# Odd layer of a hybrid decoder: values of four heads at once, tokens on partitions

## The reference

```python
h = rms_norm(x, attn_norm_g[1])
q, f, i, g = jnp.split(h @ odd_w_in[0], 4, axis=-1)      # each 256 x 2048: 16 heads of 128
f = lb + (1 - lb) * sigmoid(f); log_f = log(f); k = 1 - f
# per head, causal, in chunks: b = cumsum(log_f)
attn[t, s] = sum_d q[t, d] * k[s, d] * exp(b[t, d] - b[s, d])   # s <= t
o = attn @ i                                                    # i: the head's values, 256 x 128
o = rms_norm(o, norm_g) * silu(g)
mix = o @ odd_w_out[0]
```

## Time and profile before

| | |
|---|---|
| median of 3 runs | 2486.32 us (2485.87 to 2486.61) |
| the profiled execution, its own time | 2485.35 us |
| its span from first to last instruction | 2483.6 us |
| PE, DVE, ACT, POOL busy, share of the span | 99%, 74%, 50%, 20% |
| odd heads: products of head 0 to products of head 15 | 1283.01 to 1661.67 us |
| granted PE clock while PE works | 1.00 |

### The profile page before, as it was taken

One profiled execution on the slowest core, in us unless ns is written; L12 is line 12 of the kernel. 1 busy time (PEld: TensorE's weight loads), 2 busy tenths in 40 slices (PEclk: granted clock), 3 DMA queues, 4 the chain that ended last, 5 costly groups with the idle time before them and its releaser, 6 DMA issues.

```text
span 2483.6 us, 45860 instructions
## 1 busy us (share of the span) xinstructions
PE 2466.9 (99%) x16576; PEld 2161.3 (87%) x16576; DVE 1830.0 (74%) x3028; ACT 1237.7 (50%) x1798; POOL 504.0 (20%) x436
## 2 busy tenths in 40 slices
PE   9999999999999999999999999999999999999998
PEld 8888888888888888888888888888888888888887
DVE  7888888766665666567989999997666556655665
ACT  5666666544433444344655656555444434443444
POOL 0123322222200221022212322213222012200220
PEclk9999999999999999999999999999999999999999
DMA  7333333455555555554554444445455555555553
GB/s 274 121 138 139 121 121 121 170 186 186 194 194 187 186 186 190 192 192 170 189 184 169 169 165 172 153 163 215 178 188 187 202 186 186 186 203 185 187 195 127
DMA packets 65570, 438.32 MB, mean 176 GB/s; under 512 B 9408, under 2 KB 10816, under 8 KB 15808
## 3 DMA queue, kind: packets, MB, share of 16 engines
q1 hardware_dynamic: 61632, 436.29, 49.4%
q10 hardware_dynamic: 3840, 0.70, 0.1%
HBM read 434.87 MB, written 2.10 MB: 176 GB/s over the span
## 4 chain that ended last, share of the span: by engine, by line
PE 85%; DVE 8%; issue 4%; ACT 2%; DMA 1%; ACTq 0%; SPq 0%; DVEq 0%
PE acc L333 29%; PE acc L403 17%; PE mixer_banks L414 10%; PE acc L385 9%; PE acc L397 9%; PE acc L368 6%; DVE w_low L323 2%; DVE arena L1568 2%; DVE arena L446 1%; DVE arena L1556 1%; PE mixer_banks L1695 1%; PE acc L330 1%; DVE arena L1558 1%; DMA w_raw<-w_even 1%; PE mixer_banks L1783 0%
## 5 line engine op out<-in xcount | busy, mean ns | idle before, releaser
L318 ACT ACTIVATE w_high<-w_raw 128x1024 fp32r<-128x1024 f32 x831 | 863.3, 1057 | 892.5 <-PE acc L385 387.5
L323 DVE TENSOR_TENSOR w_low<-w_raw,w_high 128x1024 fp32r<-128x1024 f32 x832 | 1048.9, 1287 | 123.0 <-ACT w_high L318 121.7
L333 PE MATMUL acc<-h_split,w_high 128*128 128x512 f32 x3184 | 818.5, 396 | 1.0
L333 PEld LDWEIGHTS acc<-h_split,w_high 128*128 128x128 f32 x3184 | 575.3, 188 | 110.2 <-DVE arena L446 3.1
L565 POOL TENSOR_TENSOR arena<-arena,norm_scale 128x256 f32<-128x256 f32 x152 | 238.5, 1569 | 1340.9 <-DVE arena L446 1321.2
L446 DVE TENSOR_REDUCE arena<-acc 128x256 f32<-128x512 f32 x285 | 196.2, 688 | 289.3 <-PE acc L403 178.2
L403 PE MATMUL acc<-h_split,w_high 128*128 128x512 f32 x1376 | 328.2, 391 | 0.0
L403 PEld LDWEIGHTS acc<-h_split,w_high 128*128 128x128 f32 x1376 | 252.9, 188 | 48.9
L368 PEld LDWEIGHTS acc<-h_split,w_low 128*128 128x128 f32 x1824 | 263.7, 190 | 27.4
L368 PE MATMUL acc<-h_split,w_low 128*128 128x256 f32 x1824 | 273.4, 282 | 0.0
L333 PE MATMUL acc<-mix_split,w_high 128*128 128x512 f32 x752 | 185.7, 393 | 0.6 <-DVE x_residual L1140 0.6
(11 more groups left out here) (335 smaller groups left out, 2297.0 us busy)
## 6 DMA issues: line engine op xcount, KB each, us to landing
w_raw<-w_gu SPq DMA_DIRECT2D x176, 1024.0 KB, 4.8
w_raw<-w_odd SPq DMA_DIRECT2D x64, 1024.0 KB, 4.8
w_raw<-w_even SPq DMA_DIRECT2D x49, 1024.0 KB, 4.9
w_raw<-w_last SPq DMA_DIRECT2D x44, 1024.0 KB, 4.8
w_raw<-w_down SPq DMA_DIRECT2D x32, 1024.0 KB, 4.9
w_raw<-w_down SPq DMA_DIRECT2D x16, 768.0 KB, 4.3
w_raw<-w_odd_out SPq DMA_DIRECT2D x12, 1024.0 KB, 4.8
w_raw<-w_even_out SPq DMA_DIRECT2D x10, 1024.0 KB, 4.8
```

Of the source, the lines that this page charges most:

```text
L318: act.activation(wh[:, self.res, ks], raw[:, self.raw, ks], ACT.Copy).then_inc(high_done, 1)
L323: dve.tensor_tensor(wl[:, self.res, ks], raw[:, self.raw, ks], wh[:, self.res, ks].bitcast(F32), ALU.subtract).then_inc(low_done, 1)
L333: pe.matmul(acc[self.acc][:, 0:2 * T], wh[:, self.res, k], flat(both), start=k == 0, stop=stop)
```

## The change

Blocks of i are no longer one head each. Four blocks together hold the values of four heads, cut the other way: block v of a group has a quarter of the inner dimension for the 512 output columns of four heads, and is multiplied by tokens, in `by_tokens`, into two PSUM banks of the mixer that collect over four blocks. At a group's first head ACT copies both banks to `In` and multiplies by the norm's factor per token (`nrt`, which DVE makes once before the heads). So the values are not taken out by DVE, not scaled by POOL and not transposed on PE. A group's values must be complete at its first head: three blocks of the first group now run before head 0, head 0 runs the fourth and each following step a quarter of the next group. The loads keep their count, 64 blocks. Steps 0 to 12 have four blocks each, steps 13 and 14 three (f, g, q), with other cuts, and step 15 none as before. Steps 1 to 12 are a loop of three rounds over four steps; 0, 13, 14 and 15 are written out. The sigmoids of head 0 move ahead of three blocks' weight copies.

```diff
...
+        PRE = 6
+        GROUP_STEPS = NHG - 3
...
+        def odd_first(h):
...
+            return ODD + PRE + 4 * h - max(0, h - GROUP_STEPS) if isinstance(h, int) else None
...
+        def odd_block(h, u):
...
+            if isinstance(h, int):
+                first = odd_first(h)
+                return Block(first + u, kt=KT)
+            i, v = h
+            return Block(ODD + PRE + 4 + 4 * v + u, i, 16)
...
+        def odd_steps(eng, step):
...
+            step(0, 0)
+            with eng.Fori(0, 3) as i:
+                for v in range(4):
+                    step(4 * i + 1 + v, (1 + v) % 4, (i, v))
+            for h in range(GROUP_STEPS, NHG):
+                step(h, h % 4)
...
-            for u in range(3):
-                scale(ODD + u, (hf, hi, hg)[u], "hg_scaled")
-            with pool.Fori(0, NHG - 1) as h:
-                for u, dst in enumerate((hq, hf, hi, hg)):
-                    scale(Block(ODD + 3 + u, h, 4).n, dst, "hg_scaled")
-            scale(ODD + 4 * NHG - 1, hq, "hg_scaled")
+            scale(ODD, hf, "hg_scaled")
+            scale(ODD + 1, hg, "hg_scaled")
...
+            def odd_scales(h, _, at=None):
+                at = h if at is None else at
+                scale(odd_block(at, -1).n, hq, "hg_scaled")
+                if isinstance(h, int) and h == NHG - 1:
+                    return
+                scale(odd_block(at, 0).n, hf, "hg_scaled")
+                scale(odd_block(at, 2 if not isinstance(h, int) or h < GROUP_STEPS else 1).n, hg, "hg_scaled")
...
+            odd_steps(pool, odd_scales)
...
-            def odd_step(h, last=False):
-                blocks = [Block(ODD + 4 + u, h, 4) for u in range(5)]
+            def odd_step(h, quarter, where=None):
+                where = h if where is None else where
+                last = isinstance(h, int) and h == NHG - 1
+                grouped = not isinstance(h, int) or h < GROUP_STEPS
+                blocks = [odd_block(where, u) for u in range(5)]
...
-                act.wait_ge(S["hg_iT"], h + 1)
-                act.activation(flat(In), bank(5)[:, 0:256], ACT.Copy).then_inc(S["hg_In"], 1)
...
-                blocks[4].high(act, 0)
+                if grouped and quarter == 0:
+                    blocks[1].wait_half(act, 1)
+                    for th in range(2):
+                        act.activation(In[:, th], bank(2 + th), ACT.Copy, scale=nrt[:, th:th + 1]).then_inc(S["hg_In"], 1)
+                if grouped or last:
+                    blocks[4].high(act, 0)
...
-                blocks[4].high(act, 1)
+                if grouped or last:
+                    blocks[4].high(act, 1)
...
-                    act.wait_ge(S["hg_scaled"], 4 * h + 7)
+                    act.wait_ge(S["hg_scaled"], 3 * h + 5)
...
-            for u in range(3):
+            for u in range(PRE - 1):
...
-            act.wait_ge(S["hg_scaled"], 3)
-            gates()
-            with act.Fori(0, NHG - 1) as h:
-                odd_step(h)
-            odd_step(NHG - 1, last=True)
+                if u == 1:
+                    act.wait_ge(S["hg_scaled"], 2)
+                    gates()
+            act.wait_ge(S["hg_nrt"], 2)
+            odd_steps(act, odd_step)
...
-            def odd_step(h, last=False):
+            def odd_step(h, quarter, where=None):
+                where = h if where is None else where
+                last = isinstance(h, int) and h == NHG - 1
+                grouped = not isinstance(h, int) or h < GROUP_STEPS
...
-                    Block(ODD + 4 + half // 2, h, 4).low(dve, half % 2)
+                    if half < 8 or grouped or last:
+                        odd_block(where, half // 2).low(dve, half % 2)
...
-                        Block(ODD + 4 + u, h, 4).evacuate(dve, dst)
+                        odd_block(where, u if grouped else u // 2).evacuate(dve, dst, 2 if grouped and u == 0 else 1)
...
-                dve.wait_ge(S["hg_iT"], h + 1)
-                take(1, hi)
+                if last:
+                    take(1, None)
...
-            for u in range(3):
+            for u in range(PRE - 1):
...
-                Block(ODD + u).evacuate(dve, (hf, hi, hg)[u])
+                if u < 2:
+                    Block(ODD + u).evacuate(dve, (hf, hg)[u], (1, PRE - 2)[u])
...
+                if u == 1:
+                    dve.wait_ge(S["norm_rstd"], 3)
+                    turned = htmp.rearrange("p (c t) -> p c t", c=2)
+                    dve.tensor_tensor(turned, nrs.rearrange("p (c t) -> p c t", c=2), bc(ident, 2), ALU.mult).then_inc(S["hg_nrt"], 1)
+                    dve.wait_ge(S["hg_nrt"], 1)
+                    dve.reduce_sum(nrt, turned, AX.X).then_inc(S["hg_nrt"], 1)
...
-            with dve.Fori(0, NHG - 1) as h:
-                odd_step(h)
-            odd_step(NHG - 1, last=True)
+            odd_steps(dve, odd_step)
...
-            def value_turned(h):
...
-                pe.wait_ge(S["hg_scaled"], 4 * h + 2)
-                for c in range(2):
-                    prod = transposed(bank(5)[:, c * P:(c + 1) * P], hi[:, c * P:(c + 1) * P])
-                prod.then_inc(S["hg_iT"], 1)
...
-            def odd_step(h, last=False):
+            values = (bank(2), bank(3))
...
+            def odd_step(h, quarter, where=None):
+                where = h if where is None else where
+                last = isinstance(h, int) and h == NHG - 1
+                grouped = not isinstance(h, int) or h < GROUP_STEPS
+                first_cut, second_cut, third_cut, end_cut = (32, 46, 54, 64) if grouped else (24, 36, 42, 48)
...
-                        ks = range(max(first, part * HALF) % KT, (min(end, part * HALF + HALF) - 1) % KT + 1)
-                        Block(ODD + 4 + part * HALF // KT, h, 4).run(pe, ks, hs)
+                        this = odd_block(where, part * HALF // KT)
+                        if grouped and part == 2:
+                            this.by_tokens(pe, values, hs, (quarter + 3) % 4, 4)
+                        elif not grouped or part != 3:
+                            ks = range(max(first, part * HALF) % KT, (min(end, part * HALF + HALF) - 1) % KT + 1)
+                            this.run(pe, ks, hs)
...
                 prod.then_inc(S["hg_mm"], 1)
-                dense(32, 46)
+                dense(first_cut, second_cut)
                 out_half(2, 0)
...
                 pe.wait_ge(S["hg_AT"], 4 * h + 4)
-                waits(pe, h + 1, "hg_A01", "hg_In")
-                pe.matmul(bank(5)[:, 256:384], AM[:, 0], In[:, 0], start=True, stop=True)
-                pe.matmul(bank(5)[:, 384:512], A01, In[:, 0], start=True, stop=False)
-                pe.matmul(bank(5)[:, 384:512], AM[:, 1], In[:, 1], start=False, stop=True).then_inc(S["hg_o"], 1)
-                dense(46, 54)
+                pe.wait_ge(S["hg_A01"], h + 1)
+                if quarter == 0:
+                    pe.wait_ge(S["hg_In"], 2 if isinstance(h, int) else 2 * where[0] + 4)
+                mine = slice(quarter * P, quarter * P + P)
+                pe.matmul(bank(5)[:, 256:384], AM[:, 0], In[:, 0, mine], start=True, stop=True)
+                pe.matmul(bank(5)[:, 384:512], A01, In[:, 0, mine], start=True, stop=False)
+                pe.matmul(bank(5)[:, 384:512], AM[:, 1], In[:, 1, mine], start=False, stop=True).then_inc(S["hg_o"], 1)
+                dense(second_cut, third_cut)
                 out_half(3, 0)
...
                 prod.then_inc(S["hg_oT"], 1)
-                if not last:
-                    value_turned(h + 1)
-                dense(54, 64)
+                dense(third_cut, end_cut)
                 out_half(3, 1)
-            for n in range(2, 4):
-                for half in range(2):
-                    Block(ODD + n).products(pe, half, hs)
-            pe.wait_ge(S["hg_scaled"], 2)
-            for c in range(2):
-                first_turn = transposed(bank(5)[:, c * P:(c + 1) * P], hi[:, c * P:(c + 1) * P])
-            first_turn.then_inc(S["hg_iT"], 1)
-            with pe.Fori(0, NHG - 1) as h:
-                odd_step(h)
-            odd_step(NHG - 1, last=True)
+            for q in range(3):
+                Block(ODD + 2 + q).by_tokens(pe, values, hs, q, 4)
+            for half in range(2):
+                Block(ODD + PRE - 1).products(pe, half, hs)
+            odd_steps(pe, odd_step)
             pe.wait_ge(S["hg_end"], NHG + 1)
...
-    wo = blocks(odd_w_in[0]).reshape(4, NHG, P, KT, P)
-    w_odd = wo[[1, 2, 3, 0]].transpose(1, 0, 2, 3, 4).reshape(4 * NHG, P, KT, P)
+    wq, wf, _, wg = blocks(odd_w_in[0]).reshape(4, NHG, P, KT, P)
+    wi = a(odd_w_in[0])[:, 2 * D:3 * D].reshape(4, 4, P, 4, 512).transpose(3, 0, 2, 1, 4).reshape(NHG, P, KT, P)
+    w_odd = [wf[0], wg[0], wi[0], wi[1], wi[2], wq[0]]
+    for h in range(NHG - 1):
+        w_odd += [wf[h + 1], *wi[h + 3:h + 4], wg[h + 1], wq[h + 1]]
+    w_odd = np.stack(w_odd)
...
```

(13 more changed lines are left out.)

5 lines of the change are left out of this document (2 added, 3 removed).

## The result

The changed kernel takes **2506.69 us** (median of 4 runs, 2505.83 to 2507.93), the kernel before 2486.10 (4 runs): ratio 1.0083, 95% interval 1.0071 to 1.0095. It is slower, as forecast, but by 20.6 us where +6.3 was forecast, and outside the range that was given.

The account below looks back on a forecast made before the run. Both PE's work and the cycle through PE, ACT and DVE were taken to bind. Terms: +10.38 - 0.2 - 3.9 + 0 = +6.3 us, 2492.6 us against the median of 2486.3; range 2487.5 to 2498.

Parts of the forecast that it names:

- Ahead of the heads, +10.38: Between block ODD + 1 and head 0's products: 32.96 us of PE work instead of 22.58, so +10.38.
- The small term of -0.2: At head 0: f is already taken out, so PE's 0.21 us wait is gone once, -0.2.
- Steps 0 to 12 at 0 us each: Four-block steps: PE loses 0.34 us, but nothing removed lies on the cycle, so 0 us per step.
- The rival of the longer loop: Jumps back on DVE and ACT: fetching the four-step body stalls, up to +6, estimate +3, 2495.6 us; chance 0.08.
- Steps 13 and 14, -3.9: Three-block steps: the cycle itself is cut by 1.94 us per step, -3.9 for two, and PE idles.
- The rival of the clock: Products of heads 13 and 14: PE's idle time lowers the clock, up to +8.4, estimate half, 2497 us; chance 0.10.
- The two rivals as alternatives: The clock falls at heads 13 and 14 (chance 0.10); the longer loop stalls at its jumps back (chance 0.08).
- Faster: Wait for `hg_X` in each step: PE work decides everywhere, all removed PE work counts, 5.4 us, giving 2480.9; chance 0.08.
- the steps do shorten: Steps 1 to 12: PE is the bound, 0.34 us comes off 12 times, -4.1, giving +2.2, 2488.5 us; chance 0.18.
- 23.4 us of ACT, DVE and PE's handover: One beat's chain, read as without a gap, as argument against Faster, which needs the cycle under 24.7 us.

Follow-up runs that it names:

- the padded kernel: Changed kernel with three heads in VectorE's loop body and 26 needless one-column writes per head, as long as four heads' body: 2511.62 us.

## Why the prediction was wrong

**Ahead of the heads, +10.38: right.** Measured +10.39, from two rows each. The small term of -0.2 is there too: the first beat is 25.02 us where it was 25.30.

**Steps 0 to 12 at 0 us each: right for the work, wrong for the loop.** The beats without a stall are 25.26 to 25.38 against a mean of 25.29, although PE does less. The reason given holds as well: moving the cut shortens the cycle, and only then does the beat follow. But "I cost it at 0 us per step" took the loop as free at its jumps. **This is the step that failed.** VectorE's two jumps back cost 7.9 us directly and 3.8 (2.48 + 1.35) in clock.

**The rival of the longer loop: right mechanism, wrong size.** It was put at 1.5 us a jump and engine, estimate +3, from the slowest handover by waiting. A handover says nothing about a fetch. The stall is 5 us, on VectorE alone, and with the clock 11.3 us were measured for the pair in the kernel before. The chance of 0.08 rested in part on "no loop here is as long as the new one", which was a reason to expect the unknown, not to discount it.

**Steps 13 and 14, -3.9: right, and taken back.** PE's idle time was put at 3.2 and 4.0 us; it was 2.93 and 3.95. With the clock held, the beats from heads 13 and 14 sum to 45.90 against 49.97 before, -4.07. In the changed kernel the low clock adds 1.45 and 2.84 us behind those two gaps, and the sum is 50.08. The rival of the clock, "half of +8.4", put this at 4.2; measured 4.3. That it came so near is in part luck: with one head in VectorE's loop the two falls cost 3.0 (48.90 against 45.90), and in the padded kernel the first did not come at all.

**The two rivals as alternatives: wrong.** They were given chances of 0.10 and 0.08 as if one excluded the other. They add, and the one causes the other: a stalled VectorE leaves PE idle for 3 us, and that lowers the clock twice more. The Trainium skill, "TensorE: Matmul & The Clock Gate", Part 1, has the low level as the default that activity lifts; the trace agrees at four places (2.93 to 3.95 us of idle time, then L333 at 3.2 to 3.8 us instead of 2.1). With the gaps filled down to 1.0 and 1.5 us there is no fall at heads 13 and 14. With both priced as measured the sum is 10.4 - 4.4 + 7.9 + 8.1 = 22.0. A range for rivals that add would have reached 6.3 + 6 + 8.4 = +20.7, even with the two prices as they were put.

**Faster, and "the steps do shorten": fell**, as argued; the beat stayed that of the cycle. One reading in that argument is off: "23.4 us of ACT, DVE and PE's handover" is the sum up to `XX` with PE's own 14 tiles in it (5.00 + 0.87 + 6.12 + 11.46 = 23.45). Nothing hangs on it, since the whole cycle of 25.24 is over the 24.7 that it is held against.

Still open: where between 233 and 310 records the limit is, whether it moves with the place of the code, and what besides the gap decides whether the clock falls and for how long (6.8 us behind the first jump, 3.4 behind the second, after gaps of 3.04 and 3.03).

## What to carry to other kernels

Before a loop is lengthened, look at which engine would fetch its body again: on VectorE up to 233 records went round for nothing and 310 cost 5 us at each jump back, in bodies that all begin at nearly the same place within a packet, while TensorE's body of four heads went round without a gap; where a table needs four cases, only the engines that use the case need the long body. A gap of 3 us in PE's stream can cost more than its length, since the work behind it mostly ran at low clock here, so a step that loses dense work gains only if the chain behind it shrinks too. Rivals that can hold together are to be added up, not weighed against each other.

## What was unexpected of the hardware

The stall at a jump back was all or nothing, 4.7 to 5.2 us for bodies of 310 to 318 records on VectorE, at every jump. Products that nobody reads, 19 of them, made a kernel 2.3 us faster by its median, by holding PE's clock over two gaps. And the clock fell behind a gap of 1.9 us in three traces of fourteen, but not behind one of 2.93.
